# HGRN2 mixer of a decoder trunk: the input projection in another order of columns, and the heads in steps of three half projections

## The chip, the cores and the metric

The kernel runs on one core of a Trainium2 chip. The metric is the device time of one execution in microseconds (us), lower is better. TensorE is called PE in the profile, VectorE DVE, ScalarE ACT, GpSimd POOL, SyncE SP.

## The reference, cut to what matters

Two layers over 256 tokens of width 1024. Each is a SwiGLU block, a mixer and a second SwiGLU block, with a scaled residual and a layer norm behind each. The kernel's stages are F0, AB, F1, F2, C, F3. Only stage C, the HGRN2 mixer of the second layer, is touched:

```python
def hgrn2_mixer(x, w_in, w_o, g_norm, lower_bound):
    q, fz, i, g = jnp.split(x @ w_in, 4, axis=-1)        # w_in: 1024 x 4096
    q = jax.nn.silu(q)
    f = lower_bound + (1.0 - lower_bound) * jax.nn.sigmoid(fz)
    log_f = jnp.log(f); k = 1.0 - f
    o = hgrn2_chunk_scan(heads(q), heads(k), heads(i), heads(log_f))   # 8 heads of 128
    o = rms_norm(o, g_norm).reshape(B, S, D_MODEL) * jax.nn.silu(g)
    return o @ w_o
```

The scan gives token t of a head the sum over s <= t of q_t k_s v_s, damped by the product of the f between them. All is float32.

## The kernel before, in words

**Matrix products.** Each weight and each activation is split into a float32r high part and its remainder; a product is three matmuls, hi x hi, hi x lo, lo x hi (L1196 to L1199). SP loads the weights in units of 2048 columns (1 MB) into three `raw` buffers. ACT makes the high part (`split_hi`, L371), then DVE the remainder (`split_lo`, L663), into rings of six; PE waits for `lo_ready`. A chunk is 512 columns of the input weight, two units. Projecting one chunk for one half of the tokens (t = 0 or 1, 128 tokens) is 24 matmuls of 512 columns; FIRST and SECOND are its halves, 12 matmuls each. t = 0 lands in PSUM bank G[0], t = 1 in G[1].

**Order.** Every engine has its instructions in a list written out by hand, and works through it in order; semaphores join the lists. No planner moves anything.

**Stage C.** The eight chunks come in four groups of two heads each: chunk (g, 0) holds queries and forget values of group g (256 + 256 columns), chunk (g, 1) values and gates. After a query and forget chunk ACT takes the sigmoid (L545) and DVE makes queries, keys and forget factors (L980 to L989, five kinds of instruction); ACT's `log_decay` takes the logarithm when both t are there, and DVE's `logf_split` its remainder. After a value and gate chunk ACT copies the values and takes the gates' sigmoid (L552, L553), and DVE multiplies (L995).

A head hd goes through these steps:

- `head_kqT`: PE transposes keys and queries into bank[0] (L1516), ACT copies them out (L602);
- `head_exponents`: PE makes sums of log f for nine decay patterns (L1532, L1533), ACT's `head_exp` exponentiates two banks (L609), DVE's `head_factors` multiplies in keys and queries (L1036, L1045);
- `head_levels`: PE multiplies 2 x 7 blocks (L1545), transposes one (L1553) and makes the state (L1556); DVE's `head_scores` gathers the blocks with 14 predicated copies (L1055, L1068);
- `head_outputs`: PE (L1565 to L1567); ACT squares (L624), POOL takes the root (L1164), DVE's `head_out` multiplies root and gate in (L1084);
- `head_oT`: for each pair of heads PE transposes (L1579), and ACT and DVE split (`oT_split`, L630, L1093), before the output projection `out_rows`.

PE has `head_outputs` of the last head and `head_exponents` of the next in one place, a whole projection (24 matmuls), `head_levels`, and a whole projection again: four half projections to a head. With the last projection head 5 is done; heads 6 and 7 go on between output rows. Then stage F3 begins with `xT` (L1192), which needs the layer norm of t = 0 (L680 to L710).

Of the kernel before, what the change touches and what calls it, by code (L numbers as in the profile page):

```python
# [17 lines left out]
ALU = mybir.AluOpType  # L18
# [7 lines left out]
P = 128  # L26
# [39 lines left out]
def build(nc, x, positions, ln_gain, ln_bias, ffn1_w_in, ffn1_w_out, ffn2_w_in, ffn2_w_out, ab_w_in, ab_w_o,  # L66
          diff_lambda, diff_subln, pool_w, pool_scale, c_w_in, c_w_o, c_norm, hgrn_gamma, consts, out):
    with ExitStack() as ctx:
# [3 lines left out]
        def sem(name):  # L72
# [69 lines left out]
            "qf_sigmoids", "q_ready", "f_ready", "logf_hi", "logf_lo", "val_ready", "gate_sigmoid", "gate_ready",  # L142
# [5 lines left out]
            "head_done", "head_squares", "head_rms", "head_ready", "headT_done", "headT_hi", "headT_lo")}  # L148
# [8 lines left out]
        SLOTS = [((0, 0), (1, 0), (0, 1), (1, 1))] + [((0, 0), (0, 1), (1, 0), (1, 1))] * (GROUPS - 1)  # L157
        C_CHUNKS = tuple((g, j) for g in range(GROUPS) for j in range(2))
# [95 lines left out]
        val = region(1536, 2, TT, 256)  # L254
        gate = region(2560, 2, TT, 256)
# [18 lines left out]
        def _(sp):  # L274
# [21 lines left out]
            for name in ORDER:  # L296
# [22 lines left out]
                else:  # L319
                    w_in, w_out, order = ((ab_w_in[0], ab_w_o[0], AB_CHUNKS) if name == "AB"  # L320
                                          else (c_w_in[0], c_w_o[0], C_CHUNKS))
                    for j, c in enumerate(order):
                        for kh in range(2):
                            n = s0 + 2 * j + kh
                            if name == "C":
                                load_halves(n, n, w_in, kh, 4, 2 * c[1], c[0])
                                continue
                            sp.wait_ge(lo_ready, n - RAW + 1)
                            for k in range(0, 4, 2):
                                sp.dma_start(  # L330
                                    raw[:, n % RAW, k * 512:(k + 2) * 512].rearrange("p (k f) -> p k f", k=2),
                                    w_in.rearrange("(k p) f -> p k f", p=P)[:, 4 * kh + k:4 * kh + k + 2,
                                                                            c * 512:(c + 1) * 512]
                                ).then_inc(raw_landed[n % RAW], 16)
# [13 lines left out]
        def _(act):  # L348
# [177 lines left out]
            def mix_c(m):  # L526
                s0 = phases["C"]
                k = CHUNKS_BEFORE["C"]
                xT_split(m, 0)
                for g in range(GROUPS):  # L530
                    par = g % 2
                    for slot, (j, t) in enumerate(SLOTS[g]):
                        split_hi(s0 + AHEAD + 4 * g + slot)
                        if g == 0 and slot == 0:
                            xT_split(m, 1)
                        if g == 0 and slot == 3:
                            log_decay(g)
                            head_kqT(0)
                        act.wait_ge(chunk_done[t], k + 2 * g + j + 1)
                        src = G[j] if g == 0 else G[t]  # L540
                        if j == 0:
                            if g:
                                act.wait_ge(S["kqT_done"], 2 * g)
                                act.wait_ge(S["logf_lo"], g)
                            nc.scalar.activation(qf[:, t], src.rearrange("p (a f) -> p a f", a=2), ACT.Sigmoid  # L545
                                                 ).then_inc(S["qf_sigmoids"], 1)
                        else:
                            if g == 0:
                                act.wait_ge(S["bound_ready"], 1)
                            if g >= 2:  # L550
                                act.wait_ge(S["head_ready"], 4 * (g - 1))
                            nc.scalar.copy(val[:, par, t], src[:, 0:256]).then_inc(S["val_ready"], 1)  # L552
                            nc.scalar.activation(gate[:, par, t], src[:, 256:512], ACT.Sigmoid  # L553
                                                 ).then_inc(S["gate_sigmoid"], 1)

                        hd = (4 * g + slot - 3) // 2
                        if hd < 0:
                            continue
                        if hd == 6:
                            oT_split(0)  # L560
                            head_squares(5)
                            oT_split(1)
                            head_exp(6)
                            head_kqT(7)
                        elif slot % 2:
                            head_exp(hd)
                            if hd:
                                head_squares(hd - 1)
                            if hd % 2 == 0:
                                head_kqT(hd + 1)  # L570
                        else:
                            if hd % 2:
                                head_kqT(hd + 1)
                            head_state(hd)
                            if slot == 2:
                                log_decay(g)

                oT_split(2)
                head_state(6)
                split_hi(s0 + AHEAD + 16)  # L580
                split_hi(s0 + AHEAD + 17)
                head_exp(7)
                head_squares(6)
                split_hi(s0 + AHEAD + 18)
                head_state(7)
                head_squares(7)
                oT_split(3)
                split_hi(s0 + AHEAD + 19)
# [15 lines left out]
            def head_exp(hd):  # L604
                act.wait_ge(S["exponents_done"], 2 * hd + 2)
                if hd:
                    act.wait_ge(S["head_done"], hd)
                for b in range(2):
                    nc.scalar.activation(fac[:, 4 * b:4 * b + 4].rearrange("p l t f -> p t l f"),  # L609
                                         levels_both[:, :, b].rearrange("p t (l f) -> p t l f", l=4), ACT.Exp  # L610
                                         ).then_inc(S["decays_ready"], 1)
# [7 lines left out]
            def head_squares(hd):  # L619

                act.wait_ge(S["head_done"], hd + 1)
                for t in range(TT):
                    col = 2 * (hd % 2) + t
                    nc.scalar.activation(bank[1][:, (2 + t) * P:(3 + t) * P], bank[1][:, t * P:(t + 1) * P],  # L624
                                         ACT.Square, accum_out=ssq[:, 0, col:col + 1]).then_inc(S["head_squares"], 1)

# [22 lines left out]
        def _(dve):  # L649
# [307 lines left out]
            def mix_c(m):  # L957
# [3 lines left out]
                for g in range(GROUPS):  # L961
                    par = g % 2
                    for slot, (j, t) in enumerate(SLOTS[g]):
                        if slot == 3 and g:
                            logf_split(g)
                        split_lo(s0 + AHEAD + 4 * g + slot)
                        src = G[j] if g == 0 else G[t]
                        if g == 0 and slot == 0:

                            dve.wait_ge(x_ready, 4 * m)  # L970
                            nc.vector.tensor_copy(ln_gb[:], gam).then_inc(S["bound_ready"], 1)
                            xT_split(m, 1)
                            dve.wait_ge(S["bound_ready"], 1)
                        if slot == 3 and g == 0:
                            logf_split(g)
                        if j == 0:
                            gs = slice(g * 256, (g + 1) * 256)
                            rest, lb, f = ln_gb[:, 0, gs], ln_gb[:, 1, gs], logf[:, t]
                            dve.wait_ge(S["qf_sigmoids"], 2 * g + t + 1)
                            nc.vector.tensor_tensor(q_tok[:, t], q_tok[:, t], src[:, 0:256], ALU.mult  # L980
                                                    ).then_inc(S["q_ready"], 1)
                            step(nc.vector.tensor_tensor(f, f, rest, ALU.mult))
                            step(nc.vector.tensor_tensor(k_tok[:, t], rest, f, ALU.subtract))

                            nc.vector.scalar_tensor_tensor(out=f, in0=f, scalar=1e-18, in1=lb,
                                                           op0=ALU.max, op1=ALU.add).then_inc(S["f_ready"], 1)
                            for h in range(2):
                                hs = slice(h * P, (h + 1) * P)
                                ins = nc.vector.tensor_tensor_reduce(  # L989
                                    out=kq_tmp[:, h], in0=k_tok[:, t, hs], in1=q_tok[:, t, hs], scale=1.0, scalar=0.0,  # L990
                                    op0=ALU.mult, op1=ALU.add, accum_out=kq_own[:, par, t, h:h + 1])
                            step(ins)
                        else:
                            dve.wait_ge(S["gate_sigmoid"], 2 * g + t + 1)
                            nc.vector.tensor_tensor(gate[:, par, t], gate[:, par, t], src[:, 256:512], ALU.mult  # L995
# [647 lines left out]
```

## Time and profile before

| | us |
|---|---|
| three runs | 1039.02, 1039.26, 1041.03; median 1039.26 |
| the profiled execution | 1038.74 |
| its span, first to last instruction | 1036.6 |
| PE busy | 1005.6 |
| DVE busy | 653.4 |
| ACT busy | 495.7 |

The span leaves 2.1 us of the profiled execution outside it. Stage C's own work on PE begins about 672 us into the span and ends with L1192 at 840.35. A matmul's listed duration overlaps the next one's; its cost in a stream is the distance from one start to the next, and "idle before" is the time in which the engine had nothing running.

### The profile page before, as it was taken

Reading aid. Unit: us, or ns where it says so; the run is one execution under the profiler, and the core shown is the slowest. Engines: PE = TensorE matmul, PEld = TensorE weight load, DVE = VectorE, ACT = ScalarE, POOL = GpSimd, SP = SyncE. Lnnn points to the kernel's source line nnn. Section 1 sums busy time; section 2 is a strip of 40 time slices with the busy share of each in tenths; the row PEclk is TensorE's granted clock in tenths of the full one; section 3 lists DMA queues with packets and bytes.
Section 4 is the critical chain, followed back from the end, with each engine's and each line's share of the span. In section 5 each row is a group of like instructions: output and inputs, shape, how many; then the busy total and the mean of one; then the engine's idle time right before and its main releaser. Section 6 shows DMA issues by size and latency. Waiting matters only on the chain.

```text
span 1036.6 us, 12902 instructions
## 1 busy us (share of the span) xinstructions
PE 1005.6 (97%) x4748; PEld 832.8 (80%) x4748; DVE 653.4 (63%) x837; ACT 495.7 (48%) x548; POOL 33.0 (3%) x61
## 2 busy tenths in 40 slices
PE   5999999999999999999999999999999899999997
PEld 4888888887788888888888888888888778888885
DVE  4564454886777545567954455878877876454555
ACT  4455454336547444452534335286777335334340
POOL 2000000000210000000000000000000100000000
PEclk9999999999999999999999999999999999999999
DMA  9765555553655665574476565453433346555531
GB/s 311 267 203 186 188 179 199 180 187 107 235 202 182 226 201 176 189 230 134 164 242 196 172 198 184 143 168 117 132 111 122 104 147 231 186 184 202 166 118 40
DMA packets 133108, 184.29 MB, mean 178 GB/s; under 512 B 5840, under 2 KB 112992, under 8 KB 132944
## 3 DMA queue, kind: packets, MB, share of 16 engines
q1 hardware_dynamic: 130160, 173.56, 50.6%
q0 software_dynamic: 2624, 9.66, 2.6%
q10 hardware_dynamic: 288, 0.59, 0.2%
q8 instruction: 23, 0.38, 0.2%
q14 instruction: 13, 0.11, 0.0%
HBM read 182.73 MB, written 1.05 MB: 177 GB/s over the span
## 4 chain that ended last, share of the span: by engine, by line
PE 89%; DVE 6%; ACT 3%; DMA 1%; issue 1%; SPq 0%; DVEq 0%; ACTq 0%
PE psum L1197 27%; PE psum L1199 27%; PE psum L1198 27%; DVE w_lo L663 2%; PE psum L1263 2%; PE psum L1545 2%; DMA raw<-in_ffn_w_in 1%; ACT w_hi L371 1%; PE psum L1192 1%; PE psum L1532 1%; PE psum L1533 1%; DVE stats L682 1%; DVE x_tok L680 1%; ACT L553 0%; ACT arena L501 0%
## 5 line engine op out<-in xcount | busy, mean ns | idle before, releaser
L663 DVE TENSOR_TENSOR w_lo<-raw,w_hi 128x2048 fp32r<-128x2048 f32 x164 | 374.9, 2290 | 182.1 <-ACT w_hi L371 181.7
L1197 PE MATMUL psum<-w_hi,xT_hi 128*128 128x512 f32 x960 | 382.5, 398 | 5.9 <-DVE xT_lo L670 4.2
L1199 PE MATMUL psum<-w_hi,xT_lo 128*128 128x512 f32 x960 | 375.2, 391 | 0.0
L1198 PE MATMUL psum<-w_lo,xT_hi 128*128 128x512 f32 x960 | 375.1, 391 | 0.0
L371 ACT CAST w_hi<-raw 128x2048 fp32r<-128x2048 f32 x164 | 311.8, 1908 | 14.7 <-DMA raw<-in_ffn_w_in 10.4
L1197 PEld LDWEIGHTS psum<-w_hi,xT_hi 128*128 128x128 f32 x960 | 181.0, 189 | 43.9 <-DVE xT_lo L670 5.1
L1199 PEld LDWEIGHTS psum<-w_hi,xT_lo 128*128 128x128 f32 x960 | 180.8, 188 | 39.1
L1198 PEld LDWEIGHTS psum<-w_lo,xT_hi 128*128 128x128 f32 x960 | 181.1, 189 | 35.5
L381 ACT ACTIVATE ffn_tok<-psum 128x256 f32<-128x256 f32 x88 | 33.8, 384 | 241.4 <-PE psum L1199 241.3
L1197 PE MATMUL psum<-w_hi,hT_hi 128*128 128x512 f32 x352 | 138.3, 393 | 0.0
L1199 PE MATMUL psum<-w_hi,hT_lo 128*128 128x512 f32 x352 | 137.2, 390 | 0.0
L1198 PE MATMUL psum<-w_lo,hT_hi 128*128 128x512 f32 x352 | 137.0, 389 | 0.0
L721 DVE TENSOR_TENSOR ffn_tok<-psum,ffn_tok 128x256 f32<-128x256 f32 x88 | 37.2, 423 | 84.3 <-ACT ffn_tok L381 84.2
L385 ACT CAST hT_hi<-psum 128x512 fp32r<-128x512 f32 x40 | 23.5, 587 | 125.2 <-PE psum L1263 125.2
L1197 PEld LDWEIGHTS psum<-w_hi,hT_hi 128*128 128x128 f32 x352 | 66.1, 188 | 14.6 <-DVE hT_lo L791 1.3
L1199 PEld LDWEIGHTS psum<-w_hi,hT_lo 128*128 128x128 f32 x352 | 66.1, 188 | 13.9
L1198 PEld LDWEIGHTS psum<-w_lo,hT_hi 128*128 128x128 f32 x352 | 66.1, 188 | 13.3
L725 DVE TENSOR_TENSOR hT_lo<-psum,hT_hi 128x512 fp32r<-128x512 f32 x40 | 27.6, 690 | 58.7 <-ACT hT_hi L385 58.7
L376 ACT CAST xT_hi<-psum 128x512 fp32r<-128x512 f32 x24 | 13.0, 589 | 52.1 <-PE psum L1192 52.0
L1068 DVE COPY_PREDICATED arena<-level_mask,psum 128x128 f32<-128x128 uint8 x112 | 29.9, 300 | 3.8 <-PE psum L1545 1.3
L1545 PE MATMUL psum<-arena 128*128 128x128 f32 x224 | 29.2, 285 | 2.6 <-DVE arena L1045 2.6
L1128 POOL TENSOR_TENSOR rstd<-veps,mhalf 128x1 f32<-128x1 f32 x12 | 6.7, 559 | 765.8 <-DVE veps L684 765.8
(159 smaller groups left out, 580.2 us busy)
## 6 DMA issues: line engine op xcount, KB each, us to landing
raw<-in_ffn_w_in SPq DMA_DIRECT2D x176, 512.0 KB, 4.7
raw<-in_ffn_w_out SPq DMA_DIRECT2D x88, 512.0 KB, 4.0
raw<-in_c_w_in SPq DMA_DIRECT2D x32, 512.0 KB, 4.8
raw<-in_ab_w_in SPq DMA_DIRECT2D x16, 512.0 KB, 4.8
raw<-in_ab_w_o SPq DMA_DIRECT2D x8, 512.0 KB, 3.7
raw<-in_c_w_o SPq DMA_DIRECT2D x8, 512.0 KB, 4.1
ln_gb<-in_ln_gain POOLq DMA_DIRECT2D x6, 512.0 KB, 4.9
ln_gb<-in_ln_bias POOLq DMA_DIRECT2D x6, 512.0 KB, 6.1
```

The lines of the kernel that those rows point to most:

```text
L371: nc.scalar.copy(w_hi[:, n % RING], raw[:, slot]).then_inc(hi_ready, 1)
L381: nc.scalar.activation(ffn_tok[:, 0, t], g[:, 0:FC], ACT.Silu).then_inc(silu_ready, 1)
L385: nc.scalar.copy(hT_hi[:, par], T[0]).then_inc(hidT_hi, 1)
L663: nc.vector.tensor_tensor(w_lo[:, n % RING], raw[:, n % RAW], w_hi[:, n % RING].bitcast(F32), ALU.subtract).then_inc(lo_ready, 1)
L721: nc.vector.tensor_tensor(hid, g[:, FC:2 * FC], ffn_tok[:, 0, t], ALU.mult).then_inc(hid_ready, 1)
L725: nc.vector.tensor_tensor(hT_lo[:, par], T[0], hT_hi[:, par].bitcast(F32), ALU.subtract).then_inc(hidT_lo, 1)
L1068: ins = nc.vector.copy_predicated(scT[:, t], level_mask[:, l], levels_both[:, t, l // 4, (l % 4) * P:(l % 4 + 1) * P])
L1197: nc.tensor.matmul(dst, a_hi, b_hi, start=first, stop=False)
L1198: nc.tensor.matmul(dst, a_hi, b_lo, start=False, stop=False)
L1199: return nc.tensor.matmul(dst, a_lo, b_hi, start=False, stop=last)
L1263: ins = nc.tensor.transpose(T[0][:, j * SEQ + t * P:j * SEQ + (t + 1) * P], src[:, j * P:(j + 1) * P], ident[:])
L1545: ins = nc.tensor.matmul(LV[t][:, l // 4, (l % 4) * P:(l % 4 + 1) * P], fac[:, 1 + l, t], fac[:, 1 + l, t], start=True, stop=True)
```

## The change: what it does

- The eight chunks now come as qf0, v0, qf1, qf2, v1, qf3, gate0, gate1: "v" and "gate" chunks are 512 columns of one kind, for four heads. They are loaded in two transfers of two row blocks instead of two of column halves.
- From the third chunk on work is counted in half projections (12 matmuls), number `half` = 8 to 31. Head hd has three: phase 0 (outputs of hd-1, exponents of hd), phase 1 (nothing or `head_kqT`), phase 2 (`head_levels`). Head 7's levels come with the last half.
- The gates are SiLU on ACT alone. The root is multiplied in by ACT (`head_norm`), the gate by DVE for up to four heads at once (`head_gate`).
- `head_exponents` does the first bank of both t first, and `head_exp` starts on it with two smaller instructions.
- The tail: all of out_rows for t = 0, then all for t = 1.

The diff, cut to what the prediction speaks of:

```diff
-        C_CHUNKS = tuple((g, j) for g in range(GROUPS) for j in range(2))
+        C_CHUNKS = (("qf", 0), ("v", 0), ("qf", 1), ("qf", 2), ("v", 1), ("qf", 3), ("gate", 0), ("gate", 1))
+        HALVES = range(8, 4 * len(C_CHUNKS))
+        KQT_AT = {9: 1, 13: 2, 14: 3, 17: 4, 20: 5, 25: 6, 26: 7}
+        GROUP_AT = {11: (1, 0), 12: (1, 1), 15: (2, 0), 17: (2, 1), 23: (3, 0), 24: (3, 1)}
...
 ACT
+                for half in HALVES:
+                    hd, phase = divmod(half - HALVES[0], 3)
+                    t_ended = half // 2 % 2 ^ 1
+                    kind, c = C_CHUNKS[(half - 1) // 4]
+                    evacuates = half % 2 == 0
+                    early = kind == "v" or phase
+                    if half == 18:
+                        log_decay(2)
+                    if evacuates and kind == "qf" and phase == 1:
+                        sigmoids(c, t_ended, G[t_ended])
+                    if half % 2 == 0:
+                        split_hi(s0 + AHEAD + half // 2)
+                    if evacuates and early and not (kind == "qf" and phase == 1):
+                        evacuate(kind, c, t_ended)
+                    if half in KQT_AT:
+                        head_kqT(KQT_AT[half])
+                    if phase == 0:
+                        head_exp(hd)
+                        if evacuates and not early:
+                            evacuate(kind, c, t_ended)
+                        if hd:
+                            head_squares(hd - 1)
+                    elif phase == 1:
+                        if hd:
+                            head_norm(hd - 1)
+                    else:
+                        if hd == 7:
+                            oT_split(0)
+                        head_state(hd)
+                        if hd in (1, 5):
+                            log_decay(hd // 2 + 1)
...
 DVE
+                for half in HALVES:
+                    hd, phase = divmod(half - HALVES[0], 3)
+                    if half % 2 == 0:
+                        split_lo(s0 + AHEAD + half // 2)
+                    if half in GROUP_AT:
+                        g, t = GROUP_AT[half]
+                        queries_decays(g, t, G[t])      # L980 to L989
+                    if half == 18:
+                        logf_split(2)
+                    if phase == 0:
+                        if hd == 7:
+                            head_gate(0, 1, 0, 4)
+                        head_factors(hd)
+                    elif phase == 1:
+                        if hd == 6:
+                            head_gate(0, 0, 0, 4)
+                    else:
+                        if hd == 7:
+                            oT_split(0)
+                        head_scores(hd)
+                        if hd in (1, 5):
+                            logf_split(hd // 2 + 1)
...
 PE
+                for half in HALVES:
+                    hd, phase = divmod(half - HALVES[0], 3)
+                    c, t = half // 4, half // 2 % 2
+                    if half in KQT_AT:
+                        head_kqT(KQT_AT[half])
+                    if phase == 0:
+                        if hd:
+                            head_outputs(hd - 1)
+                        head_exponents(hd)
+                    elif phase == 2:
+                        if hd == 7:
+                            head_oT(0)
+                        head_levels(hd)
+                    if half % 2 == 0:
+                        bank_read(c, t)
+                    project(s0 + 2 * c, None, t, G[t], (FIRST, SECOND)[half % 2])
+                head_outputs(7)
+                head_oT(1)
+                out_rows(u0, 0, 0)
+                head_oT(2)
+                out_rows(u0, 0, 1)
+                head_oT(3)
+                out_rows(u0, 0, 2)
+                out_rows(u0, 0, 3)
+                for j in range(3):
+                    out_rows(u0, 1, j)
+                out_rows(u0, 1, 3, hs=(0,))
...
+            def head_norm(hd):
+                act.wait_ge(S["head_rms"], hd + 1)
+                for t in range(TT):
+                    col = 2 * (hd % 2) + t
+                    nc.scalar.activation(o_half[hd // 4][:, t, (hd % 4) * P:(hd % 4 + 1) * P],
+                                         bank[1][:, t * P:(t + 1) * P], ACT.Copy, scale=ssq[:, 1, col:col + 1]
+                                         ).then_inc(S["head_ready"], 1)
```

## Rows read from the trace of the kernel before

**Rows 1.** The page: the chain that ended last, share by engine.

```profile
PE 89%; DVE 6%; ACT 3%; DMA 1%; issue 1%; SPq 0%; DVEq 0%; ACTq 0%
```

**Rows 2.** PE's waits, whole span: line, releaser, total us, times, longest.

```profile
PE psum L1545 <- DVE arena L1045: 2.6, 1, 2.6
PE psum L1565 <- issue: 2.3, 1, 2.3
PE psum L1553 <- ACT arena L602: 1.9, 3, 0.6
PE psum L1192 <- DVE x_tok L710: 1.7, 1, 1.7
...
PE psum L1579 <- DVE xT_lo L1093: 0.6, 1, 0.6
```

**Rows 3.** Stretches: length, busy and count of PE, PEld, DVE, ACT, POOL; clock, DMA.

```profile
687.28:840.35 153.07, 143.72 (x799) 123.37 (x799) 121.08 (x296) 97.57 (x137) 10.39 (x19) 0.99 0.38 124
```

**Rows 4.** The same view in steps of 2 us, about PE's two longest waits.

```profile
818.00:820.00 2.00, 2.00 (x10) 1.90 (x10) 1.01 (x5) 0.41 (x1) 0.00 (x0) 0.50 1.01 336
...
822.00:824.00 2.00, 0.19 (x2) 0.00 (x0) 1.90 (x8) 0.27 (x1) 0.00 (x0) 1.00 0.00 0
```

**Rows 5.** PE in order of time: start, us, line, idle before; projections left out.

```profile
798.00 0.63 PE L1579 MATMUL psum<-ident,ffn_tok 128*128 128x128 f32 x4 [0.56 <-DVE xT_lo L1093]
801.21 0.60 PE L1516 MATMUL psum<-ident,arena 128*128 128x128 f32 x4
...
804.85 1.73 PE L1545 MATMUL psum<-arena 128*128 128x128 f32 x14
...
808.31 0.39 PE L1556 MATMUL psum<-arena 128*128 128x128 f32 x2
811.29 0.38 PE L1565 MATMUL psum<-arena 128*128 128x128 f32 x2
...
811.87 0.48 PE L1532 MATMUL psum<-decay,hT_hi 128*128 128x512 f32 x1
...
813.70 0.40 PE L1533 MATMUL psum<-decay,hT_lo 128*128 128x512 f32 x1
816.74 3.49 PE L1545 MATMUL psum<-arena 128*128 128x128 f32 x14 [2.65 <-DVE arena L1045]
...
820.23 1.73 PE L1545 MATMUL psum<-arena 128*128 128x128 f32 x14
```

**Rows 6.** ACT in order of time, pieces of two heads.

```profile
704.41 0.60 ACT L545 ACTIVATE arena<-psum 128x512 f32<-128x512 f32 x1 [3.40 <-PE psum L1199]
705.12 1.28 ACT L609 ACT_TABLE_LOAD   x1
707.04 1.94 ACT L609 ACTIVATE arena<-psum 128x1024 f32<-128x1024 f32 x2 [0.65 <-PE psum L1533]
...
709.44 1.91 ACT L371 CAST w_hi<-raw 128x2048 fp32r<-128x2048 f32 x1
...
718.84 0.63 ACT L593 ACTIVATE arena<-arena 128x512 f32<-128x512 f32 x1
719.50 0.62 ACT L596 CAST hT_hi<-arena 128x512 fp32r<-128x512 f32 x1
```

**Rows 7.** DVE in order of time, about the same head.

```profile
699.41 0.48 DVE L1055 TENSOR_SCALAR arena<-ident,kq_own 128x128 f32<-128x128 f32 x2
699.93 3.99 DVE L1068 COPY_PREDICATED arena<-level_mask,psum 128x128 f32<-128x128 uint8 x14
703.83 2.28 DVE L663 TENSOR_TENSOR w_lo<-raw,w_hi 128x2048 fp32r<-128x2048 f32 x1
706.03 0.41 DVE L980 TENSOR_TENSOR arena<-arena,psum 128x256 f32<-128x256 f32 x1
...
707.27 0.42 DVE L985 SCALAR_TENSOR_TENSOR arena<-arena,ln_gb 128x256 f32<-128x256 f32 x1
...
708.55 2.50 DVE L1045 TENSOR_TENSOR arena<-arena 128x256 f32<-128x256 f32 x7
```

More of the change, by code:

```diff
@@ L324, in _ @@
                             n = s0 + 2 * j + kh
-                            if name == "C":
-                                load_halves(n, n, w_in, kh, 4, 2 * c[1], c[0])
+                            if name == "C" and c[0] == "qf":
+                                load_halves(n, n, w_in, kh, 4, 0, c[1])
                                 continue
+                            first = (c if name == "AB" else C_COLUMN[c[0]] + c[1]) * 512
                             sp.wait_ge(lo_ready, n - RAW + 1)
@@ L527, in mix_c @@
                 s0 = phases["C"]
-                k = CHUNKS_BEFORE["C"]
                 xT_split(m, 0)
[L530 to L559, printed above, removed]
-                            oT_split(0)
[L561 to L576, printed above, removed]
@@ new lines, in mix_c @@
+                split_hi(s0 + AHEAD)
+                xT_split(m, 1)
+                sigmoids(0, 0, G[0])
+                split_hi(s0 + AHEAD + 1)
+                act.wait_ge(S["bound_ready"], 1)
+                value(0, 0, G[1])
+                split_hi(s0 + AHEAD + 2)
+                sigmoids(0, 1, G[0])
+                split_hi(s0 + AHEAD + 3)
+                log_decay(0)
+                head_kqT(0)
+                for half in HALVES:
[25 more added lines that the diff above has]
+                        if hd == 7:
+                            oT_split(0)
+                        head_state(hd)
+                        if hd in (1, 5):
+                            log_decay(hd // 2 + 1)
@@ L578, in mix_c @@
+                evacuate("gate", 1, 1)
+                oT_split(1)
+                head_squares(7)
+                split_hi(s0 + AHEAD + 16)
+                head_norm(7)
                 oT_split(2)
-                head_state(6)
-                split_hi(s0 + AHEAD + 16)
                 split_hi(s0 + AHEAD + 17)
-                head_exp(7)
-                head_squares(6)
+                oT_split(3)
                 split_hi(s0 + AHEAD + 18)
-                head_state(7)
-                head_squares(7)
@@ L587, in mix_c, with chunk_landed, sigmoids @@
-                oT_split(3)
                 split_hi(s0 + AHEAD + 19)
+            def chunk_landed(i, t):
+                act.wait_ge(chunk_done[t], CHUNKS_BEFORE["C"] + i + 1)
+            def sigmoids(g, t, src):
+                chunk_landed(C_CHUNKS.index(("qf", g)), t)
+                if g:
+                    act.wait_ge(S["kqT_done"], 2 * g)
+                    act.wait_ge(S["logf_lo"], g)
+                nc.scalar.activation(qf[:, t], src.rearrange("p (a f) -> p a f", a=2), ACT.Sigmoid
+                                     ).then_inc(S["qf_sigmoids"], 1)
@@ new lines, in value, with gates @@
+            def value(v, t, src):
+                chunk_landed(C_CHUNKS.index(("v", v)), t)
+                nc.scalar.copy(val[v][:, t], src).then_inc(S["val_ready"], 1)
+            def gates(i, t, src):
+                chunk_landed(C_CHUNKS.index(("gate", i)), t)
+                if i == 0:
+                    act.wait_ge(S["head_done"], 4)
+                else:
+                    act.wait_ge(S["kqT_done"], 8)
+                    act.wait_ge(S["logf_lo"], GROUPS)
+                nc.scalar.activation(gate[i][:, t], src, ACT.Silu).then_inc(S["gate_ready"], 1)
@@ L604, in head_exp @@
             def head_exp(hd):
-                act.wait_ge(S["exponents_done"], 2 * hd + 2)
                 if hd:
                     act.wait_ge(S["head_done"], hd)
[L608 to L611, printed above, removed]
+                act.wait_ge(S["exponents_done"], 2 * hd + 1)
+                for t in range(TT):
+                    ins = nc.scalar.activation(fac[:, 0:4, t], LV[t][:, 0].rearrange("p (l f) -> p l f", l=4), ACT.Exp)
+                ins.then_inc(S["decays_ready"], 1)
+                act.wait_ge(S["exponents_done"], 2 * hd + 2)
+                nc.scalar.activation(fac[:, 4:8].rearrange("p l t f -> p t l f"),
+                                     levels_both[:, :, 1].rearrange("p t (l f) -> p t l f", l=4), ACT.Exp
+                                     ).then_inc(S["decays_ready"], 1)
             def head_state(hd):
@@ L960, in mix_c @@
                 norm(ORDER[m - 1], 1)
[L961 to L995, printed above, removed]
-                                                    ).then_inc(S["gate_ready"], 1)
-                        hd = (4 * g + slot - 3) // 2
-                        if hd < 0:
-                            continue
@@ new lines, in mix_c @@
+                split_lo(s0 + AHEAD)
+                dve.wait_ge(x_ready, 4 * m)
+                nc.vector.tensor_copy(ln_gb[:], gam).then_inc(S["bound_ready"], 1)
+                xT_split(m, 1)
+                dve.wait_ge(S["bound_ready"], 1)
+                queries_decays(0, 0, G[0])
+                split_lo(s0 + AHEAD + 1)
+                split_lo(s0 + AHEAD + 2)
+                queries_decays(0, 1, G[0])
+                split_lo(s0 + AHEAD + 3)
+                logf_split(0)
+                for half in HALVES:
[12 more added lines that the diff above has]
+                    elif phase == 1:
@@ L1021, in mix_c, with queries_decays @@
-                oT_split(3)
                 split_lo(s0 + AHEAD + 19)
-                norm("C", 0)
+            def queries_decays(g, t, src):
+                gs = slice(g * 256, (g + 1) * 256)
+                rest, lb, f = ln_gb[:, 0, gs], ln_gb[:, 1, gs], logf[:, t]
+                dve.wait_ge(S["qf_sigmoids"], 2 * g + t + 1)
+                nc.vector.tensor_tensor(q_tok[:, t], q_tok[:, t], src[:, 0:256], ALU.mult
+                                        ).then_inc(S["q_ready"], 1)
+                step(nc.vector.tensor_tensor(f, f, rest, ALU.mult))
+                step(nc.vector.tensor_tensor(k_tok[:, t], rest, f, ALU.subtract))
+                nc.vector.scalar_tensor_tensor(out=f, in0=f, scalar=1e-18, in1=lb,
+                                               op0=ALU.max, op1=ALU.add).then_inc(S["f_ready"], 1)
+                for h in range(2):
+                    hs = slice(h * P, (h + 1) * P)
+                    ins = nc.vector.tensor_tensor_reduce(
+                        out=kq_tmp[:, h], in0=k_tok[:, t, hs], in1=q_tok[:, t, hs], scale=1.0, scalar=0.0,
+                        op0=ALU.mult, op1=ALU.add, accum_out=kq_own[:, g % 2, t, h:h + 1])
+                step(ins)
@@ L1526, in head_exponents @@
                 hi, lo = (h[:, g % 2].rearrange("p (t f) -> p t f", t=TT) for h in (hT_hi, hT_lo))
-                for t in range(TT):
-                    for b, d0, d1 in (((0, 0, 4), (1, 4, 8)) if t == 0 else ((0, 8, 9), (0, 1, 4), (1, 4, 8))):
+                for b, parts in ((0, ((0, 0, 4), (1, 8, 9), (1, 1, 4))), (1, ((0, 4, 8), (1, 4, 8)))):
+                    for t, d0, d1 in parts:
                         c0 = P if (d0, d1) == (1, 4) else 0
```

158 lines of the change are left out of this document (60 added, 98 removed).

## The prediction, made before the changed kernel was run

> **What bounds the kernel now.** First the chain that ended last: PE holds 89% of it [rows 1], so a stage is worth on PE what PE does in it and what PE waits for. Then PE's waits over the whole span: apart from the start of the kernel and stage AB, the ones that count lie in stage C, 2.6 + 2.3 + 1.9 + 1.7 + 0.6 us [rows 2], four of the five in its tail. Then the stretch from the first exponents (687.28) to F3's first transposes (840.35): 153.07 us, with DVE busy 121.08 and ACT 97.57 [rows 3]. DVE works 79% of it, so a schedule that packs PE tighter soon meets it.
>
> **What the change leaves of PE's work.** Starts in PE's list give the prices: four transposes and a half projection 801.21 - 798.00 = 3.21; levels 808.31 - 804.85 = 3.46 (a copy in front included) and 0.14 for the state, 3.4 where nothing is late; state and half projection 811.29 - 808.31 = 2.98, so a half costs 2.84 and four transposes 0.37; outputs 811.87 - 811.29 = 0.58; exponents 813.70 - 811.87 + 0.23 for the last = 2.06 [rows 5]. A half that follows another without head work between costs about 0.1 less, 2.73.
> The new list from the same point, without a wait: 24 halves, 17 at 2.84 and 7 at 2.73, are 67.4; eight heads at 2.06 + 3.4 + 0.58 are 48.3; seven `head_kqT` and four `head_oT` at 0.37 are 4.1; output rows up to `xT` are 4 + 3.5 times a half-sized stream, 20.6. Sum 140.4. The stretch takes 153.1 now, so 12.7 us are there to be won: 9.1 are the waits of [rows 2], 1.5 the low clock after one of them (below), the rest restarts. The tail really loses its waits: the norm of t = 0, for which F3 waits 1.7 now, gets 3.5 rows of t = 1 (9.6 us) as its cover instead of 1.5.
>
> **What it adds: waits, one by one.** A head has 3 halves between its steps instead of 4, a period of 2.06 + 3.4 + 0.58 + 0.3 + 8.4 = 14.8 us. Levels to outputs is 2.84 instead of 5.6, and everything in order in ACT's and DVE's lists between them has to fit.
>
> *Half 13, `head_kqT(2)`.* It needs the second forget chunk's t = 1 (keys and forgets), whose projection ends with half 11. Between lies half 12 alone, 2.73 us. The chain: 0.2 to ACT, sigmoid 0.60 (up to 0.4 late, as squares and a table load of 1.28 come first); then ACT's `split_hi` 1.91 [rows 6], which stands behind this sigmoid; DVE's `split_lo` 2.28, which stands ahead of `queries_decays` and needs that high part; then L980 to L985, 707.27 + 0.42 - 706.03 = 1.66 [rows 7]; 0.2 back to PE. Together 6.85 to 7.1, so PE stands 4.1 to 4.4. I take 4.4. Behind the waiting transposes are levels of head 1 and all projections. Neither engine's idle time can absorb it, because the chain begins at PE's own half 11.
> *Half 25, `head_kqT(6)`,* the same list for group 3: 4.2.
> *Half 17, `head_kqT(4)`.* It needs group 2's t = 1, and DVE has those behind `head_scores(2)`. Counted from the start of levels(2): PE arrives at 3.4 + 2.84 = 6.2. With DVE free, scores end at 5.9 and the forgets 1.7 + 0.2 later: the least is a wait of 1.6. But `split_lo` stands ahead of the scores, and its `split_hi` on ACT stands behind `head_norm(1)`, which waits for POOL after a load, a sigmoid and the squares of half 14; it ends about 1.8 after the levels start. Then 2.28 + 0.5 + 3.99 [rows 7] + 1.7 + 0.2 make 10.5: wait 4.3. I take 4.3, the least stays as a bound.
> *Half 20:* ACT's `log_decay(2)`, 1.28 + 0.63 + 0.62 [rows 6], precedes a `split_hi`, DVE has that unit's `split_lo` and `logf_split(2)` before scores(3): 2.1. *Half 29:* `split_hi` waits behind head_norm(5) and a SiLU load; split_lo ends 4.2 after levels(6) start, plus 4.5 of scores, against PE's 6.2: 2.6. *Halves 11 and 23:* split_lo ahead of the scores, 0.5 and 0.9. *Halves 14, 26, 31 and the last `head_oT`:* 0.2, 0.1, 0.4, 0.5.
> Sum: 4.4 + 4.2 + 4.3 + 2.1 + 2.6 + 1.4 + 1.2 = 20.2. The least: 4.1 + 4.1 + 1.6 = 9.8, everything else hidden.
>
> **The clock.** After the wait of 2.65 PE ran 818 to 820 at a granted 0.50 (1.2 GHz), after the 2.33 at 822 to 824 at 1.00 (2.4 GHz) [rows 4]. At the low level 14 level matmuls from 816.74 lasted 3.49 against 1.73 [rows 5], and with the part behind them that costs about 1.5. The three waits of over 4 us are longer than the one that cost it, so I take 3 x 1.5 = 4.5; the least is 0, as the 2.33 shows, the most 6, with half 29. The Trainium skill (TensorE: Matmul & The Clock Gate, Part 1: The HAM clock gate) says that PE falls to 1.2 GHz after idle time and comes back only after sustained work. By that rule each long wait is paid twice, by the 2.33 row it is not; the first wait agrees with it.
>
> **Table loads.** Each change of function between exp, sigmoid and logarithm shows a load of 1.28 (705.12) [rows 6]. Logarithm directly followed by exp, with copies alone between, which the new list has four times, is in no row. The bounds are 0 and 1.28 each. With 1.28, ACT is later in halves 14 to 16 and 26 to 28 and PE waits some 3 more in all; copies and squares between two exps need no load, and I take 0, keeping 3 for the range.
> The Trainium skill (ScalarE: Activation LUTs, Table sets: the hidden batching unit) names a set with both exp and logarithm, so by it the 3 us do not come. The same page (What ACT_TABLE_LOAD costs) has 2.66 for a switch with its drain; here the activation starts right behind the 1.28.
>
> **The rest at nothing.** `head_norm` gives ACT 16 instructions of some 0.3 and takes as much from DVE: ACT has 55 us free in the stretch, and what its place costs is in the waits above. Gate sigmoid and product become one SiLU. The split exponent banks let DVE start 0.9 earlier, but levels come two halves (5.6) after, when factors (0.4 + 2.50) are done anyway; without that cover it would be worth 0.9. The loads move the same bytes, with DMA busy at 0.38 [rows 3], and units are split five halves ahead. Nothing outside stage C moves.
>
> **Sum.** -12.7 + 20.2 + 4.5 = +12.0. The profiled execution took 1038.74 with a span of 1036.6; it becomes 1050.7, and 1051.2 on the median 1039.26, which lies 0.5 above it.
>
> **The rivals.**
> *The waits hide, faster.* If ACT and DVE, with 21% and more of their time free, catch up everywhere but in the three chains, the waits are 9.8; and with the clock at its high level the sum is -12.7 + 9.8 = -2.9: 1036.4. For it: the tail's waits go with certainty, and the clock didn't fall after 2.33. Against: unit splits stand ahead of the scores in every second head. It decides whether waits add to more or less than 12.7. Chance 0.14.
> *A draw:* waits of about 13 and no low clock, 1039: 0.08.
> *Waits as taken, no low clock:* +7.5, 1046.8: 0.18.
> *The forecast,* 1048.5 to 1055: 0.43.
> *ACT is the bound:* loads after each logarithm (+3), the low clock after half 29 too (+1.5), and some waits longer as squares and norms back up: +16.5 and more, 1056 to 1062: 0.17. For it: ACT's list has a load and a `split_hi` ahead of nearly every step that PE waits for; against: its 55 us free.
> *It doesn't do what it says:* the order of the lists is plain, this would need a compiler that moves instructions, and no row hints at it.
>
> **How the numbers follow.** Faster by over 0.2% (2 us, about what can be told from no change here): 0.14. Within: 0.08. Slower: 0.78. The range 1039.5 to 1059 leaves out the first rival, part of the draw, and the last end of ACT as the bound, about 0.2 in all.
>
> **What would show it.** PE's waits in stage C should name L980 to L985 ahead of the transposes of `head_kqT`, twice near 4.3 and once between 1.6 and 4.3; the granted clock 0.5 behind them; the wait on L710 and the two long ones of heads 6 and 7 gone; waits of `head_outputs` on the predicated copies of 0.5 to 2.6. A steady period of 14.8 us between heads without such waits, or transposes of `head_kqT` that start at once, would make the prediction wrong at its root.

## The result, and the profile after

The changed kernel takes 1059.3 us (median of four runs, 1059.07 to 1060.88) against 1039.66 for the kernel before on the same chip: ratio 1.0193, 95% interval 1.0176 to 1.021. It is slower, as forecast, but by 20 us and not by 12, and 0.3 us above the range. The profiled execution took 1060.88, the longest of the four, with a span of 1058.8, 22.2 more than the span before; what is read from the traces below adds up to these 22, where the medians lie 20 apart. All of it lies between the first exponents and F3's transposes: that stretch is 175.62 us, 153.07 before [rows 3]. From F3's transposes to the end it is 196.1, as before.

The chain by engine, where [rows 1] has PE at 89%:

```profile
PE 84%; ACT 6%; DVE 5%; issue 2%; DMA 2%; POOL 0%; SPq 0%; DVEq 0%; ACTq 0%
```

PE's waits of the changed kernel, over the whole span (line, releaser, total, times, longest). L1533 is the transposes of `head_kqT`, L1585 `head_outputs`, L1574 the state:

```profile
PE psum L1533 <- issue: 15.0, 3, 5.3
...
PE psum L1585 <- issue: 7.1, 4, 2.9
...
PE psum L1574 <- ACT arena L642: 1.4, 2, 0.8
...
PE psum L1571 <- DVE xT_lo L1125: 0.8, 1, 0.8
```

The 1.7 for the norm and the 2.6 for the factors of head 7 [rows 2] are gone. "issue" only says that the view found no releaser: several waits stand in front of these instructions. The releaser is found by reading DVE's list up to that time, below.

The stretch in the view by windows, of the changed kernel (columns as in [rows 3]):

```profile
687.04:862.66 175.62, 151.28 (x800) 130.20 (x800) 116.97 (x279) 97.90 (x152) 10.14 (x19) 0.94 0.29 98
```

As many PE instructions as before (800, before 799), but 151.28 busy instead of 143.72, and a clock of 0.94 instead of 0.99: PE not only waits more, it also runs slower where it runs. DVE has 4.1 less to do and ACT the same.

**Half 13, read line by line.** Three lists of the changed kernel in order of time (start, us). ACT from the exponents' first bank on (PE ends that bank at about 703.5):

```profile
703.73 1.28 ACT L633 ACT_TABLE_LOAD   x1 [4.74 <-PE psum L1550]
705.02 1.09 ACT L633 ACTIVATE arena<-psum 128x512 f32<-128x512 f32 x2
705.99 1.04 ACT L636 ACTIVATE arena<-psum 128x1024 f32<-128x1024 f32 x1
...
707.60 1.28 ACT L595 ACT_TABLE_LOAD   x1
708.90 0.60 ACT L595 ACTIVATE arena<-psum 128x512 f32<-128x512 f32 x1
709.39 1.89 ACT L376 CAST w_hi<-raw 128x2048 fp32r<-128x2048 f32 x1
```

DVE behind it, unit split and then keys (L1047 to L1052):

```profile
711.31 2.29 DVE L699 TENSOR_TENSOR w_lo<-raw,w_hi 128x2048 fp32r<-128x2048 f32 x1 [2.22 <-ACT w_hi L376]
713.52 0.41 DVE L1047 TENSOR_TENSOR arena<-arena,psum 128x256 f32<-128x256 f32 x1
...
714.76 0.42 DVE L1052 SCALAR_TENSOR_TENSOR arena<-arena,ln_gb 128x256 f32<-128x256 f32 x1
```

PE, which has projected since 704.42 and is idle from 710.0 on:

```profile
715.29 1.09 PE L1533 MATMUL psum<-ident,arena 128*128 128x128 f32 x4 [5.26 <-issue]
716.17 3.19 PE L1562 MATMUL psum<-arena 128*128 128x128 f32 x14
719.16 0.42 PE L1571 MATMUL psum<-ident,arena 128*128 128x128 f32 x1
719.37 2.36 PE L1562 MATMUL psum<-arena 128*128 128x128 f32 x14
```

It is the chain of the prediction: sigmoid, high part, remainder, keys, transposes. What the prediction did not have is the first line. The table load stands behind the exponents' first bank, and it pushes everything behind it, so the sigmoid starts 1.75 after its projection's end (707.15) instead of 0.2 to 0.6. Behind the wait 14 level matmuls last 3.19 and then 2.36, where [rows 5] has 1.73. The view by windows shows the clock, here for half 13 and about half 20:

```profile
712.00:714.00 2.00, 0.00 (x0) 0.00 (x0) 2.00 (x3) 0.00 (x0) 0.00 (x0) 0.96 0.00 0
714.00:716.00 2.00, 0.71 (x4) 0.74 (x5) 1.90 (x9) 0.00 (x0) 0.00 (x0) 0.50 0.62 212
...
720.00:722.00 2.00, 2.00 (x16) 1.98 (x15) 1.24 (x6) 0.01 (x1) 0.00 (x0) 0.83 0.00 0
...
762.00:764.00 2.00, 0.02 (x1) 0.00 (x0) 1.90 (x9) 0.69 (x2) 0.00 (x0) 1.00 0.70 268
764.00:766.00 2.00, 1.46 (x8) 1.40 (x9) 1.97 (x3) 0.00 (x0) 0.00 (x0) 0.76 0.04 8
766.00:768.00 2.00, 2.00 (x8) 1.81 (x7) 0.62 (x1) 0.32 (x1) 0.00 (x0) 0.50 0.15 35
```

**The account.** From the starts in PE's list, each step less its price without a wait (all in us; the last column is what the steps behind the wait take above their price at full clock):

| half, step | wait forecast | wait measured | low clock behind it |
|---|---|---|---|
| 11 outputs | 0.5 | 0.5 | |
| 13 `kqT(2)` | 4.4 | 5.4 | 2.65 |
| 16, 28 state | 0 | 1.0 + 0.85 | |
| 17 `kqT(4)` | 4.3 | 4.7 | 1.5 |
| 20 outputs | 2.1 | 2.8 | 1.6 |
| 23 outputs | 0.9 | 1.6 | |
| 25 `kqT(6)` | 4.2 | 5.4 | 1.7 |
| 29 outputs | 2.6 | 3.0 | 1.65 |
| 31, head 7's levels | 0.4 | 1.1 | |
| 14, 26, last `oT` | 0.8 | 0.1 | |
| sum | 20.2 | 26.4 | 9.1 |

With the 140.4 of work without a wait: 175.9, measured 175.6.

### The profile page after: what moved, and what is told of

The parts are those of the page before. It is cut to its first block, busy times and chain, and to the rows that moved or that the text cites. A ratio compares the mean times of both kernels' runs of the same rounds, so it can differ in the third digit from the quotient of the medians.

```text
span 1058.8 us, 12901 instructions
## 1 busy us (share of the span) xinstructions
PE 1013.1 (96%) x4748; PEld 839.6 (79%) x4748; DVE 648.3 (61%) x819; ACT 495.1 (47%) x561; POOL 32.8 (3%) x61
## 4 chain that ended last, share of the span: by engine, by line
PE 84%; ACT 6%; DVE 5%; issue 2%; DMA 2%; POOL 0%; SPq 0%; DVEq 0%; ACTq 0%
PE psum L1229 26%; PE psum L1231 26%; PE psum L1230 26%; ACT w_hi L376 2%; DVE w_lo L699 2%; PE psum L1562 2%; PE psum L1295 2%; DMA raw<-in_ffn_w_in 1%; PE psum L1224 1%; PE psum L1549 1%; PE psum L1550 1%; ACT L633 1%; DMA raw<-in_c_w_in 1%; ACT L595 0%; ACT arena L506 0%
## 5 line engine op out<-in xcount | busy, mean ns | idle before, releaser
L1231 PEld LDWEIGHTS psum<-w_hi,hT_lo 128*128 128x128 f32 x352 | 66.1, 188 | 13.9
L1562 PEld LDWEIGHTS psum<-arena 128*128 128x128 f32 x224 | 30.3, 214 | 0.4
```

The costliest lines, as they stand in the source:

```text
L1231: return nc.tensor.matmul(dst, a_lo, b_hi, start=False, stop=last)
L1562: ins = nc.tensor.matmul(LV[t][:, l // 4, (l % 4) * P:(l % 4 + 1) * P], fac[:, 1 + l, t], fac[:, 1 + l, t], start=True, stop=True)
```

## The experiments

The theory: the pace of three halves is sound and its work on PE is as forecast; a handful of places in ACT's and DVE's lists, where a unit split or a table load stands ahead of what PE waits for, make the waits, and the longer ones cost the clock. The rival: DVE and ACT are too full for the pace, and whatever stands first, PE waits. All kernels are compared by the ratio to the kernel before, run beside them, and by the stretch from PE's first `head_kqT` to F3's transposes: 156.3 us before, 178.9 in the changed kernel. The ratio's interval of four of them (waits swapped, work in the waits, transposes later, no logarithm) overlaps that of the changed kernel, 1.0176 to 1.021: of these it doesn't show by itself that they are faster, and the reading rests on the stretch, which comes from one trace each. Where one kernel was traced on two chips (all orders), the stretch was 145.9 and 146.0.

**The two waits of `head_exp` in the other order.**

```diff
-                if hd:
-                    act.wait_ge(S["head_done"], hd)
                 act.wait_ge(S["exponents_done"], 2 * hd + 1)
+                if hd:
+                    act.wait_ge(S["head_done"], hd)
```

> The changed kernel with the two waits ahead of head_exp's first activation written in the other order, so that the table load stands behind the outputs of the last head instead of behind the exponents. Load theory (the late load of 1.28 pushes squares, sigmoid and unit split back): the load starts some 1.3 before the exponents' first bank is done, PE's waits ahead of the transposes of head_kqT in halves 13 and 25 go from 5.26 to about 4.6, the wait at half 20 from 2.5 to about 1.3; in all 3 to 5 us less than the 1059.3 of the changed kernel, 1054.3 to 1056.3. Rival (DVE's unit split ahead of everything sets the waits, ACT has time to spare): under 1 us less.

Ratio 1.0139 (1.0099 to 1.018), stretch 173.6: 5.3 less. In both traces the load starts when the wait that is written last is met: the one for the exponents (L1550) in the changed kernel, the one for `head_outputs` (L1587) here. ACT now:

```profile
703.49 1.28 ACT L633 ACT_TABLE_LOAD   x1 [3.72 <-PE psum L1587]
704.78 1.09 ACT L633 ACTIVATE arena<-psum 128x512 f32<-128x512 f32 x2
```

Halves 13 and 25 wait 1.0 less each (the expectation had 0.7), half 20 1.1 less, and 20 no longer loses the clock (1.6); half 23 0.6 less. The load theory holds. The kernel before writes the two waits in this order too, exponents first; it is the changed kernel that turned them round.

**Keys ahead of the unit split on DVE, halves 12 and 24.**

```diff
-                    if half % 2 == 0:
-                        split_lo(s0 + AHEAD + half // 2)
                     if half in GROUP_AT:
                         g, t = GROUP_AT[half]
                         queries_decays(g, t, G[t])
+                    if half % 2 == 0:
+                        split_lo(s0 + AHEAD + half // 2)
```

> The changed kernel with DVE's queries_decays ahead of split_lo in halves 12 and 24. Chain theory (PE waits in halves 13 and 25 for sigmoid, split_hi, split_lo, queries_decays in a row): both waits go from 5.26 to about 1.5, and the low clock behind them (2.6 and 1.7 us) goes with them: 10 to 12 us less, 1047 to 1049. If the clock stays low behind the shorter wait, 7.6 less: 1051.7. Rival (the keys are late because DVE is full, whatever stands first): the waits stay above 4 and the time within 2 us of 1059.3.

Ratio 1.0075 (1.0048 to 1.0101), stretch 165.0: 13.9 less, by one exchange in the source. PE's transposes and levels of half 13:

```profile
712.13 0.63 PE L1533 MATMUL psum<-ident,arena 128*128 128x128 f32 x4 [1.27 <-issue]
712.59 1.73 PE L1562 MATMUL psum<-arena 128*128 128x128 f32 x14
...
714.27 1.73 PE L1562 MATMUL psum<-arena 128*128 128x128 f32 x14
```

The waits of halves 13 and 25 go from 5.26 to 1.27 and the levels are at their old 1.73. The chain is what made these waits, and DVE was not full. That the stretch falls by 2 more than expected is the clock: it stays up behind halves 20 and 29 too, at waits of 2.2 and 2.9. Why it does so there, and fell at 2.5 and 2.9 in the changed kernel, no run shows.

**Work in the waits.** 18 matmuls of 512 columns into bank[0], overwritten by the transposes behind them.

```diff
+                if hd in (2, 4, 6):
+                    pe.wait_ge(S["state_ready"], hd - 1)
+                    for _ in range(18):
+                        nc.tensor.matmul(bank[0], decay[:, 0], decay[:, 0:4].rearrange("p l f -> p (l f)"),
+                                         start=True, stop=True)
                 pe.wait_ge(S["q_ready"], 2 * g + 2)
```

> The changed kernel with 18 matmuls of 512 columns (some 4.1 us, results overwritten) put on PE in each of the three waits ahead of head_kqT 2, 4 and 6. Clock theory (idle time of over 4 us costs the clock, and that costs 2.6 + 1.5 + 1.7 us behind the three waits): granted clock 1.00 at 714 to 722, 745 to 748 and 796 to 799, about 5.8 us less, 1053.5. Rival (levels and transposes are slow there for another reason, or the clock falls by the hour and not by idle time): the same time as the changed kernel within 1 us, or up to 1 more from the added work.

Ratio 1.0153 (1.0108 to 1.0197), stretch 173.5: 5.4 less, although PE has 54 matmuls more. Half 13:

```profile
711.66 4.24 PE L1527 MATMUL psum<-decay 128*128 128x512 f32 x18
717.10 0.63 PE L1538 MATMUL psum<-ident,arena 128*128 128x128 f32 x4 [1.19 <-issue]
717.56 1.73 PE L1567 MATMUL psum<-arena 128*128 128x128 f32 x14
```

The transposes of half 13 start 31.5 us after the stretch's start, as in the changed kernel, so the filler delays nothing. The clock is 1.00 behind all three waits (716 to 720, 744 to 748, 792 to 796) and the levels last 1.73. So the 5.8 that the changed kernel lost behind these three waits are the clock's, and come from PE's idle time. Behind half 29, which has no filler, the low clock cost 2.9 here and 1.65 in the changed kernel, at the same wait.

**Scores ahead of the unit split, halves 10, 16, 22, 28.**

```diff
-                    if half % 2 == 0:
+                    if half % 2 == 0 and phase != 2:
                         split_lo(s0 + AHEAD + half // 2)
...
                         head_scores(hd)
+                        if half % 2 == 0:
+                            split_lo(s0 + AHEAD + half // 2)
```

> The changed kernel with DVE's split_lo behind head_scores instead of ahead of it in halves 10, 16, 22 and 28. Order theory (the unit split ahead of the scores makes PE late in halves 11, 17, 23 and 29): waits there go from 0.5, 4.5, 1.5, 2.9 to 0, about 1.6, 0, 0, and the low clock behind 17 and 29 (1.5 and 1.65) goes: 10 to 11 us less, about 1048.5. Rival (DVE at 79% of the stretch is the bound, and the same split is waited for one step later): under 4 us less, with new waits of levels or exponents.

Ratio 1.0106 (1.0066 to 1.0146), stretch 170.1: 8.8 less. The waits of halves 11, 23 and 29 are gone, half 17's is 2.5 instead of 4.7, not the 1.6 expected, and it costs no clock. DVE's list shows what is left there:

```profile
734.81 3.99 DVE L1106 COPY_PREDICATED arena<-level_mask,psum 128x128 f32<-128x128 uint8 x14
738.70 2.28 DVE L699 TENSOR_TENSOR w_lo<-raw,w_hi 128x2048 fp32r<-128x2048 f32 x1
740.90 0.41 DVE L1049 TENSOR_TENSOR arena<-arena,psum 128x256 f32<-128x256 f32 x1
```

The unit split, moved behind the scores, still stands ahead of group 2's keys (L1049 here), and DVE works through without a break; the sigmoid that the keys need had ended at 736.9. Half 20 waits as before, and behind half 25 the low clock cost 2.7 instead of 1.7, at the same wait. Neither the theory's number nor the rival's: the order counts, and this exchange put only half of it right.

**`head_kqT(4)` one half later:** `KQT_AT = {..., 18: 4, ...}`.

> The changed kernel with head_kqT(4) in half 18 instead of 17, so that PE meets outputs(2) and exponents(3) first. Two waits stand one behind the other here: for scores(2), late by unit split 11, and for the keys of group 2 behind them. Theory: only the second is taken away, PE stands about 3.0 instead of 4.5 in half 17; 1.5 less, or 3.0 less if the shorter wait spares the low clock. Rival (the scores are on time, the keys alone are late): the whole 4.5 + 1.5 goes, 6 less.

Ratio 1.0173 (1.0149 to 1.0198), stretch 175.2: 3.7 less. Half 17 still waits 3.1, now with `head_outputs(2)`, and still loses the clock; half 20 gains the rest. Two waits stood one behind the other, and the late scores were the larger part of them.

**The logarithm left out.**

```diff
-                step(nc.scalar.activation(logf, logf, ACT.Ln))
+                step(nc.scalar.activation(logf, logf, ACT.Copy, scale=-1.0))
```

> The changed kernel with the logarithm of the forget factors left out (a copy with scale -1 in its place), which takes away ACT's table loads of 1.28 for it and the load of the exp table right behind it (the trace of the changed kernel shows one after each logarithm). If ACT's lateness in halves 16, 20 and 28 comes from these loads: the two waits of the state's copy, 0.8 and 0.6, go, and the wait at half 20 goes from 2.5 to about 1.2, in all 3 to 5 us less than the changed kernel. Rival (loads are hidden by ACT's free time): under 1 us less.

Ratio 1.017 (1.0146 to 1.0194), stretch 174.0: 4.8 less, the size expected and not the places. The waits of the state's copy (levels 4.41 and 4.23 us long) went only to 4.27 and 4.07. ACT's last table ahead of the logarithm is the sigmoid's, so the exp needs a load with or without it (727.38 here, 727.15 in the changed kernel), and only the logarithm's own load went. What came back is half 20: 1.2 of wait, 1.6 of clock, and 0.8 at half 23. The late state has another cause, below.

**Three orders together.**

> The changed kernel with three of the orders together: the two waits of head_exp swapped, queries_decays ahead of split_lo in halves 12 and 24, split_lo behind head_scores in halves 10, 16, 22 and 28. If the parts add up (4.5, 12 and 9 us alone against the changed kernel's stretch of 178.9 us from the first transposes to F3's): 153 to 155 us in the stretch, a ratio to the kernel before of 0.995 to 1.000. If they overlap, as each only moves PE to the next late step: 160 or more, ratio above 1.003.

Ratio 0.9945 (0.9925 to 0.9965), stretch 151.0. Alone they gave 5.3 + 13.9 + 8.8 = 28.0, together 27.8. They add up, and the kernel is 0.5% faster than the one before.

**All orders.** Besides these, splits behind the scores in phase 1 too, `head_kqT(4)` in half 18, and ACT's state ahead of the unit:

```diff
+                    if phase == 2:
+                        if hd == 7:
+                            oT_split(0)
+                        if half in KQT_AT:
+                            head_kqT(KQT_AT[half])
+                        head_state(hd)
+                        if hd in (1, 5):
+                            log_decay(hd // 2 + 1)
                     if half % 2 == 0:
                         split_hi(s0 + AHEAD + half // 2)
...
+                    if phase == 2:
+                        continue
```

> The changed kernel with every order on its waiting steps: swapped waits of head_exp, queries_decays first, split_lo behind head_scores in all of phases 1 and 2, head_kqT(4) in half 18, and in phase 2 ACT's head_state and log_decay ahead of split_hi and the evacuation. Theory (the pace of three halves is sound, the orders were not): waits of about 1 each at halves 13 and 25, under 1 at 31, no low clock; the stretch from the first transposes to F3's 147 to 149 us against 156.3 before and 178.9 in the changed kernel; ratio to the kernel before 0.991 to 0.994. Rival (DVE and ACT are too full for three halves): the stretch above 156 and the ratio above 1.

1027.1 us, ratio 0.9883 (0.9862 to 0.9903): 1.2% faster than the kernel before and 3% than the changed one, a little better than expected. Its stretch from the first exponents, by the view by windows:

```profile
687.02:829.67 142.65, 140.98 (x800) 121.94 (x799) 116.44 (x279) 98.12 (x152) 12.55 (x19) 1.00 0.36 121
```

PE is busy 140.98 of 142.65 us at full clock. The state's waits are gone (levels 3.37). With three orders, where `split_hi` and the sigmoid still stand ahead of the state's copy on ACT, they were there (0.73 and 0.59), so that place is the likely cause; it was not moved alone. All that PE still waits for in stage C:

```profile
PE psum L1537 <- issue: 1.5, 2, 0.8
```

**The norm's cover taken away** from this kernel:

```diff
+                out_rows(u0, 1, 0)
+                out_rows(u0, 1, 1)
                 out_rows(u0, 0, 3)
-                for j in range(3):
-                    out_rows(u0, 1, j)
+                out_rows(u0, 1, 2)
                 out_rows(u0, 1, 3, hs=(0,))
```

> The kernel all_orders with its tail's output rows in another order: t = 1's first two rows ahead of t = 0's last, so that the layer norm of t = 0 has 1.5 rows (4.1 us) behind it on PE instead of 3.5 rows, as in the kernel before. Cover theory: the norm takes 6.2 us from the last rows of t = 0, so the transposes of F3 wait about 2.1 us, and the time rises by 2 from 1027.1 to 1029, the ratio to the kernel before from 0.988 to 0.990. Rival (the norm is no longer late, because DVE's splits around it have moved): no wait there and the same time as all_orders.

> The kernel all_orders again, beside the run with the short cover on the same chip, so that a difference of 2 us can be told: the same ratio to the kernel before as in its first run, 0.986 to 0.990.

The short cover has 0.9949 (0.9928 to 0.997), the kernel again 0.9877 (0.9855 to 0.9899): 7.4 us between the medians, not 2. The transposes wait 0.23 and not 2.1; the price is one step later, at F3's first projection (all PE, in order of time):

```profile
832.18 1.32 PE L1228 MATMUL psum<-ident,x_tok 128*128 128x128 f32 x8 [0.23 <-DVE x_tok L749]
...
837.85 0.69 PE L1233 MATMUL psum<-w_hi,xT_hi 128*128 128x512 f32 x1 [2.95 <-DVE xT_lo L709]
838.34 0.63 PE L1234 MATMUL psum<-w_lo,xT_hi 128*128 128x512 f32 x1
```

Two unit splits (832.70 to 837.19) stand between DVE's norm and its split of the transposed x, and the projection then starts at 0.50 clock. The spans differ by 6.7: 0.3 of it lies in the stretch and 5.0 behind F3's transposes (201.1 to the end against 196.1); 1.3 lies ahead of the stretch, where the edit changes nothing. So the long tail of t = 1 is worth about 5 us with this order of splits. The kernel before has its norm behind all unit splits; what the cover is worth there was not run.

## Why the prediction was right in sign and too small

Two terms of the sum failed. The waits, "= 20.2", measured 26.4, above all because a table load stood where the prediction did not have it; and the low clock behind them, "3 x 1.5 = 4.5", measured 9.1. Together they are 10.8 above the forecast, more than the 8 between the medians' 1051.2 and 1059.3 (the trace is of the longest execution).

- **PE's work:** 140.4 forecast; the kernel with all orders has 142.65 with 1.5 of named waits in it. Right within 1 us, so the 12.7 us were there to be won.
- **Half 13, half 25:** the chain and its releaser as forecast, 4.4 and 4.2 against 5.4 each. The step that failed is "up to 0.4 late, as squares and a table load of 1.28 come first": the prediction had the exp's load done before the exponents, as the row at 705.12 shows it [rows 6], while the changed kernel's load waits for them, because its two waits are written in the other order; the sigmoid started 1.75 behind its projection's end. Swapping the two waits gives the 1.0 back. (The terms of the chain add up to 7.25 with the 0.4, not 7.1; this changes the wait by 0.15.)
- **Half 17:** 4.3 against 4.7, and the two causes that it named are both shown: the late scores alone hold PE for 3.1 with the transposes later, the keys behind them for the rest.
- **Halves 20, 23, 29 and the state:** 5.6 forecast, 9.25 measured. Of this, the late load makes 1.1 at half 20 and 0.6 at half 23, as swapping the waits shows. The state's copy behind `split_hi`, forecast at 0, is 1.85. Loads between a logarithm and the next exp were taken as 0 with 3 kept for the range: the trace has one each time (727.15, between copies and exp). No run takes this load away alone, so what it costs stays open. The Trainium skill (ScalarE: Activation LUTs, Table sets: the hidden batching unit) names a set with both functions; the 1.28 at 727.15 shows that this program doesn't use it.
- **The clock, the step that failed most:** the term "3 x 1.5 = 4.5" measured 9.1. There were five falls, not three: halves 20 and 29 (2.5 and 2.9 idle) had one too, which the prediction kept for its upper rival in half 29 alone. And the one behind half 13 cost 2.65, because it lasted from 714 to past 720, while the one seen before ended within 3.5. `filled_waits` shows that at three of the five PE's idle time is the cause. The Trainium skill (TensorE: Matmul & The Clock Gate, Part 1: The HAM clock gate) says that PE falls to 1.2 GHz after idle time and comes back after sustained work. The five falls agree; but a wait of 2.88 with a fall and one of 2.89 without (half 29, here and with keys first) show that the length of a wait alone does not tell.
- **The tail:** its waits went, as forecast. With all orders about 5 us hung on its cover, where 2 were expected.
- **The rivals:** the faster one had the least waits of 9.8 and needed every other one hidden; 16.6 us more came. The upper one, "ACT is the bound", had 1056 to 1062 and a chance of 0.17, and the measured 1059.3 lies in it. Its loads came and the fall after half 29 too, but ACT is not the bound: it was no less busy with all orders (98.12 us), and PE hardly waited. Where its work stood was.

## What to carry to other kernels

Before work is packed tighter, walk for each wait of the busiest engine the instructions that stand ahead of its releaser in the other engines' lists, and put filler (here the unit splits, needed only five halves later) behind the urgent step: a few such exchanges turned +1.9% into -1.2%, with the same work. They were not tried on the kernel before, so how much of the 1.2% belongs to the pace of three halves and how much to the orders is open. As an estimate from this case, a wait of several us on PE costs nearly half as much again in clock (9.1 behind five waits of 21.3 together). Where an activation changes the table, look in the trace which of its waits the load waits for.

## What the runs showed of the hardware

- The clock falls behind some waits and not behind others of the same length: behind 2.65 [rows 5], 2.52 (half 20) and 2.88 (half 29, both in the changed kernel) it fell to 0.50; behind 2.33 [rows 4], 2.33 (half 17 with scores first) and 2.89 (half 29 with keys first) it did not. Behind all waits of 4.2 and more in the stretch it fell. How long it stays low differs too, 3 to 7 us, and with it the price, 1.5 to 2.9 us.
- A table load is an instruction of its own in ACT's list. It can start before its activation's operand is there (703.49 with the waits swapped) or be held until it is (703.73 in the changed kernel, 1.0 later counted from the stretch's start), by the order in which two waits are written; worth 5.3 us of the stretch here.
